# Opening of a two-layer hybrid DeltaNet and diffusion step on one Trainium2 core: x in four loads, squares summed on TensorE, first modulation in fp32 by column groups, first two weight units in two rounds of four k-tiles

## Chip, cores and metric

The kernel runs on one core of a Trainium2 chip. The metric is the device time of one execution in microseconds (us); three runs of the kernel before gave a median of 1513.23 us (1513.16 to 1515.1).

## What is computed

Two groups of tokens, 512 latent and 128 context tokens of width 1024, go through two layers with the same weights. Only the very beginning matters here:

```python
x_lat = x_sample + sincos_2d(rows, GRID_W, D_MODEL)
mod = silu(cond) @ w_ada[layer] + b_ada[layer]
shift1, scale1, gate1, shift2, scale2, gate2 = split(mod, 6)
h = rmsnorm(x, norm_mix_g[layer]) * (1 + scale1) + shift1
p = h @ w_in
```

`cond` is one vector per group (two in all), so `mod` has two columns. After that come a short convolution, a gated delta rule, the output projection, a convolutional feed-forward, and the second layer.

## The kernel before

All activations lie transposed: channels on the 128 partitions, tokens along the free axis. `x` is `[128, 8, 640]`, that is 8 k-tiles of 128 channels by 640 tokens (512 latent, 128 context). A product of full accuracy is made of three fp32r products: each weight tile and each activation is split into a high part (a rounding to fp32r) and a low part (the rest), and TensorE adds hi·hi, hi·lo and lo·hi. A *unit* is one 128-column block of a weight matrix, 8 k-tiles long; it takes 8 k-tiles x 3 products x 2 halves of 320 tokens = 48 matmuls (`products`, L682). The input projection has units 0 to 27.

The opening, everything ahead of unit 0, runs so. SyncE issues one queue of DMAs in this order (L460 to L470): `cols` (small constants, 343.5 KB), the position tables, all of `x` in one transfer (2560 KB), `const`, the first 16 column tiles of `w_ada` in four transfers of 2048 KB each, the first two units of `w_in` (`raw`, 512 KB each), then `cond_rows` and two row tiles. VectorE adds the positions tile by tile (L1549), ScalarE squares each tile (L1051) and VectorE adds the squares to `acc` (L1416), two tiles in flight. TensorE sums `acc` and the last square over the partitions with a matrix of ones in fp32 (`norm_sums(0)`, L714); ScalarE makes `rstd` from it (L1020, L1022).

The first modulation (shift1 and scale1 of layer 0) is worked out in 16 steps: ScalarE rounds a slot of 1024 weights per partition (`ada_hi`, L1066), VectorE subtracts (L1576), TensorE multiplies with 4 stationary columns, the two conditions in high and low parts (`ada`, L694, 8 matmuls of 256 columns a slot). After each pair of slots ScalarE copies the 4 rows out of PSUM (L1072) and TensorE turns them into columns with small fp32 matmuls against `sel` (`ada_columns`, L705). There are four pairs of split buffers, and `ada_hi(n)` waits for the matmuls of slot n-4.

Then ScalarE and VectorE split the weights of units 0 and 1 (L1090, L1570), VectorE multiplies x by `rstd` (L1475), adds the bias and folds the norm gain (L1462, L1468), ScalarE scales and shifts tile by tile (`modulate`, L1036) and rounds (L1043), and VectorE forms the low part (L1479). Unit 0 waits for each k-tile as it comes; unit 1 follows with all eight there. Behind it ScalarE's program has the SiLU of `cond_rows` (L1094), and then for each unit `take` (PSUM to SBUF, L1101), `weight_hi` (L1112) and `silu` (L1106); VectorE's has `conv` (L1514 to L1523), `weight_lo(u + 2)` (L1570) and from unit 1 on a row sum (L1500). Unit u + 2 can begin when its weights are split:

```python
for u in range(NQK):
    take(u, u % 2, u)
    weight_hi(u + 2)
    silu(u % 2, u, u)
```

Of the kernel before, what the change touches and what calls it, by code (L numbers as in the profile page):

```python
# [26 lines left out]
P = 128  # L27
D = 1024
KD = D // P
# [6 lines left out]
HALF = W // 2  # L36
# [5 lines left out]
ADA_COLS = 2 * P  # L42
# [27 lines left out]
for _name, _n in (("norm_mix", 2 * KD * 2), ("norm_ffn", 2 * KD * 2), ("pool_scale", KD * 2),  # L70
                  ("final", KD), ("tap_qkv", 3 * NQKV), ("tap_b", 3 * NB), ("tap_ffn", 2 * 3 * NF),
                  ("o_norm", 1), ("a_log", NT * 8), ("dt_bias", NT * 8), ("w_ba", KD * 16),
                  ("cond", KD * 2), ("b_ada", 96 * 2), ("sel", 2)):
# [72 lines left out]
def build(nc, t):  # L146
    ctx = ExitStack()
    with ctx:
# [17 lines left out]
        silu_c = sb("silu_c", [P, KD, 2])  # L166
        c_parts = sb("c_parts", [P, 2, KD, 4], F32R)
        warm = sb("warm", [P, 1])
        ada_rows = sb("ada_rows", [4, ADA_COLS])
# [17 lines left out]
        sq = [work[:, 6, :], work[:, 7, :]]  # L187
        acc = work[:, 8, :]
# [6 lines left out]
        def heads(ap, n):  # L195
# [47 lines left out]
        ada_first = nc.alloc_sbuf_tensor_at("ada_first", [P, ADA_FIRST, SLOT], F32, offset=off_m)  # L243
        pe_tab = nc.alloc_sbuf_tensor_at("pe_tab", [P, 4, ROWS + GRID_W], F32, offset=off_h)
        more = [nc.alloc_sbuf_tensor_at(f"more{j}", [P, SLOT], F32R, offset=off_h + 2048 + j * SLOT * 4)
                for j in range(8)]
        assert ADA_FIRST * SLOT * 4 <= o4 - off_m
# [47 lines left out]
        s_x = sem("x_loaded")  # L295
# [11 lines left out]
        s_c_parts = sem("c_parts_ready")  # L307
        s_ada_hi = sem("ada_hi")
        s_ada_lo = sem("ada_lo")
# [8 lines left out]
        s_sq = sem("squares_ready")  # L318
        s_acc = sem("squares_added")
# [116 lines left out]
        def ada_row(n):  # L436

            return ps[0:4, (4, 5)[n // 2 % 2], 0:ADA_COLS]

        def ada_split(n):  # L440

            return more[n % 4], more[4 + n % 4]
# [5 lines left out]
        def _(sp):  # L448
# [13 lines left out]
            sp.dma_start(x[:], t["x"]).then_inc(s_x, 16)  # L462
            sp.dma_start(const[:], t["const"]).then_inc(s_const, 16)
            n = ADA_FIRST // 4
            for q in range(4):
                sp.dma_start(ada_first[:, n * q:n * (q + 1), :],
                             t["w_ada"][n * q:n * (q + 1)].rearrange("u p f -> p u f")).then_inc(s_ada1[q], 16)
# [204 lines left out]
        def _(pe):  # L672
# [15 lines left out]
            def ada(n):  # L688

                s = n % 2  # L690
                pe.wait_ge(s_ada_lo, n + 1)
                for k in range(4):
                    for q, w in enumerate(ada_split(n)):
                        last = nc.tensor.matmul(ada_row(n), c_parts[:, q, 4 * s + k, :],  # L694
                                                w[:, k * ADA_COLS:(k + 1) * ADA_COLS],
                                                start=(s == 0 and k == 0 and q == 0),
                                                stop=(s == 1 and k == 3 and q == 1))
                last.then_inc(s_ada_pe, 1)

            def ada_columns(g):  # L700

                pe.wait_ge(s_ada_cp, g + 1)
                for h in range(2):
                    at = ADA_COLS + 2 * (2 * g + h)
                    last = nc.tensor.matmul(ps[:, 0, at:at + 2], ada_rows[:, h * P:(h + 1) * P],  # L705
                                            col("sel")[0:4], start=True, stop=True)
                last.then_inc(s_ada_t, 1)
# [1375 lines left out]
```

## Time and profile before

| what | value |
|---|---|
| median of three runs | 1513.23 us |
| span of the profiled execution, first to last instruction | 1508.5 us |
| TensorE busy over the span | 1403.6 us (93%) |
| VectorE, ScalarE, GpSimd busy | 988.2, 430.7, 496.7 us |
| mean granted TensorE clock | 0.982 |
| DMA traffic | 163.24 MB, 31% of 16 engines |

The profiled execution's own time is given by its span; the median of the runs is 4.7 us above it, which is what lies around the span. A busy time is the sum of an engine's instructions; time in which TensorE is idle is lost only where nothing else could have been done there.

### The profile page before, as it was taken

The page shows a single profiled execution, that of the slowest core. Times are in us where ns is not written, and L with a number is a line of the kernel's source. Part 1 is how long each engine was busy: PE and PEld are TensorE (multiplying, and loading weights), DVE is VectorE, ACT ScalarE, POOL GpSimd, SP SyncE. Part 2 cuts the span into 40 slices and gives each one's busy share as a digit, 9 for nine tenths or more (in the row PEclk, how much of TensorE's full clock was granted, in tenths as well). Part 3 has the DMA queues.
Part 4 walks back from the last instruction along what each step waited for, and adds up shares of the span by engine and source line. Part 5 has one row for each costly group of instructions (what it writes and reads, how often), then busy time and mean ns, then how long its engine had stood idle before and what let it go on. Part 6 is the DMA issues. An engine that isn't in the chain of part 4 may idle for free.

```text
span 1508.5 us, 24564 instructions
## 1 busy us (share of the span) xinstructions
PE 1403.6 (93%) x9517; PEld 1366.5 (91%) x9517; DVE 988.2 (66%) x1405; ACT 430.7 (29%) x748; POOL 496.7 (33%) x300
## 2 busy tenths in 40 slices
PE   2799999989888899999999999878999999999996
PEld 1599989989788799999999999768999999999995
DVE  5774689887675777778788886447774155325554
ACT  4834443364421532102310321344110011001122
POOL 0000010003225133453356334113544545445442
PEclk9899999999989999999999999999999999999998
DMA  9342211353032244343434442111332222222222
GB/s 371 123 154 84 99 56 71 139 173 133 15 129 84 84 138 177 129 159 115 150 117 167 138 136 73 54 42 56 111 107 75 70 83 68 73 82 70 69 72 82
DMA packets 44791, 163.24 MB, mean 108 GB/s; under 512 B 4800, under 2 KB 5952, under 8 KB 43584
## 3 DMA queue, kind: packets, MB, share of 16 engines
q1 hardware_dynamic: 44736, 162.52, 31.1%
q8 instruction: 32, 0.52, 0.1%
q14 instruction: 23, 0.19, 0.0%
HBM read 154.12 MB, written 6.82 MB: 107 GB/s over the span
## 4 chain that ended last, share of the span: by engine, by line
PE 82%; DVE 8%; ACT 4%; issue 3%; DMA 2%; ACTq 0%; POOL 0%; DVEq 0%; SPq 0%; POOLq 0%
PE ps L682 73%; PE ps L967 1%; ACT work L1036 1%; ACT work L1184 1%; DMA x<-in_x 1%; PE ps L714 1%; PE ps L790 1%; DMA work<-in_zeros 1%; DVE wlo L1570 1%; PE ps L921 1%; PE ps L919 1%; PE ps L909 1%; PE ps L760 1%; PE ps L694 1%; DVE work L1416 1%
## 5 line engine op out<-in xcount | busy, mean ns | idle before, releaser
L682 PE MATMUL ps<-hhi,whi 128*128 128x320 f32 x1984 | 458.7, 312 | 29.4 <-DVE hlo L1479 27.4
L682 PE MATMUL ps<-hlo,whi 128*128 128x320 f32 x1984 | 453.9, 310 | 0.0
L682 PE MATMUL ps<-hhi,wlo 128*128 128x320 f32 x1984 | 453.2, 310 | 0.0
L682 PEld LDWEIGHTS ps<-hhi,whi 128*128 128x128 f32 x1984 | 333.6, 189 | 37.3 <-issue 23.9
L682 PEld LDWEIGHTS ps<-hlo,whi 128*128 128x128 f32 x1984 | 334.2, 189 | 0.0
L682 PEld LDWEIGHTS ps<-hhi,wlo 128*128 128x128 f32 x1984 | 333.7, 189 | 0.0
L603 POOL TENSOR_TENSOR wlo<-raw,whi 128x1024 fp32r<-128x1024 f32 (+1 forms) x100 | 249.7, 2497 | 8.3
L600 POOL TENSOR_SCALAR whi<-raw 128x1024 fp32r<-128x1024 f32 (+1 forms) x100 | 102.9, 1029 | 401.7 <-PE ps L682 360.5
L608 POOL TENSOR_TENSOR wlo<-raw,whi 128x1024 fp32r<-128x1024 f32 x44 | 110.2, 2504 | 214.2 <-ACT whi L1387 214.2
L682 PE MATMUL ps<-hidlo,whi 128*128 128x320 f32 x704 | 160.3, 308 | 0.0
L682 PE MATMUL ps<-hidhi,wlo 128*128 128x320 f32 x704 | 160.2, 308 | 0.0
L682 PE MATMUL ps<-hidhi,whi 128*128 128x320 f32 x704 | 160.2, 308 | 0.0
L1394 ACT ACTIVATE work<-ps 128x640 f32<-128x640 f32 x44 | 31.1, 706 | 429.0 <-PE ps L682 429.0
L1924 DVE TENSOR_TENSOR hidlo<-work,hidhi 128x640 fp32r<-128x640 f32 (+1 forms) x44 | 107.1, 2434 | 41.2 <-ACT hidhi L1404 41.2
L1517 DVE SCALAR_TENSOR_TENSOR work<-work,cols 128x511 f32<-128x511 f32 x120 | 122.3, 1060 | 3.7 <-DVE work L1514 0.3
L1514 DVE TENSOR_SCALAR work<-work,cols 128x640 f32<-128x640 f32 x60 | 60.2, 1003 | 97.0 <-ACT work L1394 79.5
L1500 DVE SCALAR_TENSOR_TENSOR ada_raw<-ada_raw,cond_rows 128x1024 bf16<-128x1024 f32 x70 | 121.7, 1738 | 0.0
L682 PEld LDWEIGHTS ps<-hidhi,wlo 128*128 128x128 f32 x704 | 117.8, 188 | 0.0
L682 PEld LDWEIGHTS ps<-hidlo,whi 128*128 128x128 f32 x704 | 117.8, 188 | 0.0
L682 PEld LDWEIGHTS ps<-hidhi,whi 128*128 128x128 f32 x704 | 117.7, 188 | 0.0
L1399 ACT ACTIVATE work<-work 128x640 f32<-128x640 f32 x44 | 32.5, 739 | 216.9 <-DVE work L1523 216.9
L1451 DVE SCALAR_TENSOR_TENSOR x<-ps,mod,x 128x320 f32<-128x320 f32 (+2 forms) x120 | 45.4, 434 | 70.5 <-PE ps L682 70.5
(197 smaller groups left out, 1403.6 us busy)
## 6 DMA issues: line engine op xcount, KB each, us to landing
raw<-in_w_gu SPq DMA_DIRECT2D x88, 512.0 KB, 3.2
ada_raw<-in_w_rows SPq DMA_DIRECT2D x70, 512.0 KB, 3.4
raw<-in_w_in SPq DMA_DIRECT2D x28, 512.0 KB, 3.3
raw<-in_w_dn SPq DMA_DIRECT2D x32, 448.0 KB, 3.3
ada_first<-in_w_ada SPq DMA_DIRECT2D x4, 2048.0 KB, 22.7
raw<-in_w_dn SPq DMA_DIRECT2D x16, 512.0 KB, 3.3
row_late<-in_w_rows SPq DMA_DIRECT2D x10, 512.0 KB, 3.3
raw<-in_w_out SPq DMA_DIRECT2D x8, 512.0 KB, 4.3
```

Of the source, the lines that this page charges most:

```text
L600: nc.gpsimd.tensor_scalar(whi[s][:, 0:n], raw[s][:, 0:n], 1.0, 0.0, ALU.mult, ALU.add).then_inc(s_whi, 1)
L603: nc.gpsimd.tensor_tensor(wlo[s][:, 0:n], raw[s][:, 0:n], whi[s][:, 0:n].bitcast(F32), ALU.subtract).then_inc(s_split, 1)
L608: nc.gpsimd.tensor_tensor(wlo[s][:], raw[s][:], whi[s][:].bitcast(F32), ALU.subtract).then_inc(s_split, 1)
L682: last = nc.tensor.matmul(pair[pr][:, b], wt[s][:, cs], act[:, k, b * HALF:(b + 1) * HALF], start=(j == 0 and q == 0), stop=(j == len(tile ...
L694: last = nc.tensor.matmul(ada_row(n), c_parts[:, q, 4 * s + k, :], w[:, k * ADA_COLS:(k + 1) * ADA_COLS], start=(s == 0 and k == 0 and q = ...
L1394: nc.scalar.activation(halves(pad[0]), pair["A"], ACT.Copy).then_inc(s_ev["A"], 1)
L1399: nc.scalar.activation(cv[1], cv[0], ACT.Silu).then_inc(s_silu, 1)
L1451: last = nc.vector.scalar_tensor_tensor(out=x[:, k, xc:xc + ln], in0=pair[n][:, bk, pc:pc + ln], scalar=mod[:, layer, 3 * part + 2, k, cd: ...
L1500: last = nc.vector.scalar_tensor_tensor(out=(row_out(n), row_buf(n)[:, 0:SLOT // 2].bitcast(mybir.dt.bfloat16))[c], in0=row_buf(n), scalar ...
L1514: own.tick(nc.vector.tensor_scalar(dst[:, 0:W], src[:, 0:W], taps[1], None, ALU.mult))
L1517: last = nc.vector.scalar_tensor_tensor(out=dst[:, c0 + 1:c0 + n], in0=src[:, c0:c0 + n - 1], scalar=taps[0], in1=dst[:, c0 + 1:c0 + n], o ...
L1924: nc.vector.tensor_tensor(hidlo[:, i, :], h32[0], hidhi[:, i, :].bitcast(F32), ALU.subtract).then_inc(s_hid, 1)
```

## The change

`x` comes in four transfers of two k-tiles, the first ahead of `const`; `cols` comes after `x`, then the two `raw` units, and only then `w_ada`, again in four transfers of 2048 KB, now grouped as two halves (`half`) of 4 k-tiles of shift and scale each. Positions go tile by tile as the transfers land. The squares are no longer added on VectorE: each of the 8 squared tiles is summed by TensorE in fp32 (16 matmuls instead of 4).

The split of the first `w_ada` tiles goes. `c_cols` holds the two conditions in the first 2 of 32 columns for every k-tile (the rest zeros), and fp32 matmuls of 512 columns write PSUM partitions 0, 32, 64 or 96 onward: shift or scale (`b`) times first or second half of the contraction (`part`). There are 16 of them in each half. One copy and four fp32 matmuls with `sel` (which adds the two parts) give the columns of a half; bias and fold are done per half.

Odd k-tiles are modulated by VectorE, even ones by ScalarE, all in buffers of their own. Units 0 and 1 run in two rounds: k-tiles 0 to 3 of both, then the second half of the modulation, then k-tiles 4 to 7 of unit 0 and of unit 1. `weight_lo(2)` goes ahead of the convolution of unit 0. Semaphore counts elsewhere are shifted to match.

```diff
-        silu_c = sb("silu_c", [P, KD, 2])
...
+        first_sq = sq + cv
+        first_h = pad + h32 + cv + sq
...
-        ada_first = nc.alloc_sbuf_tensor_at("ada_first", [P, ADA_FIRST, SLOT], F32, offset=off_m)
+        ada_first = nc.alloc_sbuf_tensor_at("ada_first", [P, 2, 2, 4, 2, ADA_SPAN], F32, offset=off_m)
+        ada_end = off_m + ADA_FIRST * SLOT * 4
+        ada_rows = nc.alloc_sbuf_tensor_at("ada_rows", [P, 2, ADA_SPAN], F32, offset=ada_end)
...
                 sp.sem_inc(sm, PRIMED)
+            sp.dma_start(pe_tab[:], t["pe"]).then_inc(s_pe, 16)
+            sp.dma_start(x[:, 0:2], t["x"][:, 0:2]).then_inc(s_x[0], 16)
+            sp.dma_start(const[:], t["const"]).then_inc(s_const, 16)
+            for j in range(1, 4):
+                sp.dma_start(x[:, 2 * j:2 * j + 2], t["x"][:, 2 * j:2 * j + 2]).then_inc(s_x[j], 16)
             sp.dma_start(cols[:], t["cols"]).then_inc(s_cols, 16)
-            sp.dma_start(pe_tab[:], t["pe"]).then_inc(s_pe, 16)
...
             for s in range(2):
                 sp.dma_start(raw[s][:], t["w_in"][s]).then_inc(s_raw[s], 16)
+            for half in range(2):
+                for q in range(2):
+                    sp.dma_start(ada_first[:, half, q], t["w_ada"][half, q]).then_inc(s_ada1[2 * half + q], 16)
...
-            def ada(n):
...
+            def first_sums():
+                pe.wait_ge(s_const, 16)
+                for k in range(KD):
+                    pe.wait_ge(s_sq, k + 1)
+                    for b in range(2):
+                        last = nc.tensor.matmul(pair["X"][:, b], ones, first_sq[k % 4][:, b * HALF:(b + 1) * HALF],
+                                                start=(k == 0), stop=(k == KD - 1))
+                    last.then_inc(s_first_sums, 1)
+            def ada(half):
+                for q in range(2):
+                    pe.wait_ge(s_ada1[2 * half + q], 16)
+                    for i in range(2):
+                        for b in range(2):
+                            for part in range(2):
+                                row = BLOCK * (2 * b + part)
+                                last = nc.tensor.matmul(ada_bank(half)[row:row + BLOCK], c_cols[:, 4 * part + 2 * q + i, :],
+                                                        ada_first[:, half, q, 2 * part + i, b, :],
+                                                        start=(q == 0 and i == 0), stop=(q == 1 and i == 1))
                 last.then_inc(s_ada_pe, 1)
-            def ada_columns(g):
...
+            def ada_columns(half):
+                pe.wait_ge(s_ada_cp, half + 1)
+                for i in range(4):
+                    last = nc.tensor.matmul(first_mods(half)[:, 4 * i:4 * i + 4], ada_rows[:, half, i * P:(i + 1) * P],
+                                            col("sel"), start=True, stop=True)
                 last.then_inc(s_ada_t, 1)
             def norm_sums(q):
-                for part, (src, sm, n) in enumerate(((acc, s_acc, 8 * (q + 1)), (sq[1], s_sq, 8 * (q + 1)))):
+                for part, (src, sm, n) in enumerate(((acc, s_acc, 8 * q), (sq[1], s_sq, 8 * (q + 1)))):
                     pe.wait_ge(sm, n)
                     for b in range(2):
                         last = nc.tensor.matmul(pair["X"][:, b], ones, src[:, b * HALF:(b + 1) * HALF],
                                                 start=(part == 0), stop=(part == 1))
                 last.then_inc(s_norm, 1)
-            pe.wait_ge(s_const, 16)
...
+            def first_units(s, ks):
+                for k in ks:
+                    pe.wait_ge(s_h, PRIMED + k + 1)
+                    for q, (wt, act) in enumerate(((whi, hhi), (whi, hlo), (wlo, hhi))):
+                        for b in range(2):
+                            last = nc.tensor.matmul(pair["AB"[s]][:, b], wt[s][:, k * P:(k + 1) * P],
+                                                    act[:, k, b * HALF:(b + 1) * HALF],
+                                                    start=(k == 0 and q == 0), stop=(k == KD - 1 and q == 2))
+                return last
+            first_sums()
+            pe.wait_ge(s_silu_c, 1)
+            ada(0)
+            ada_columns(0)
+            for k in range(4):
+                for s in range(2):
+                    if k == 0:
+                        pe.wait_ge(s_split, s + 1)
+                    first_units(s, [k])
+            ada(1)
+            ada_columns(1)
+            for s in range(2):
+                first_units(s, range(4, KD)).then_inc(s_unit, 1)
...
             for u in range(28):
-                in_unit(u, u // 2, u % 2, (lambda j: pe.wait_ge(s_h, PRIMED + j + 1)) if u == 0 else None)
+                if u >= 2:
+                    in_unit(u, u // 2, u % 2)
...
-            def ada_hi(n):
...
+            def weight_hi(u):
+                act.wait_ge(s_raw[u % 2], u // 2 * 16 + 16)
+                act.wait_ge(s_unit, u - 1)
+                nc.scalar.activation(whi[u % 2][:], raw[u % 2][:], ACT.Copy).then_inc(s_whi, 1)
+            def first_square(k):
+                act.wait_ge(s_x0, k + 1)
+                if k >= 4:
+                    act.wait_ge(s_first_sums, k - 3)
+                nc.scalar.activation(first_sq[k % 4], x[:, k, :], ACT.Square).then_inc(s_sq, 1)
+            def first_modulate(k):
+                act.wait_ge(s_first_fold, k // 4 + 1)
+                act.wait_ge(s_a, k + 1)
+                for c0, n, cd in RANGES:
+                    last = nc.scalar.activation(first_h[k][:, c0:c0 + n], first_h[k][:, c0:c0 + n], ACT.Identity,
+                                                bias=mod[:, 0, 0, k, cd:cd + 1], scale=mod[:, 0, 1, k, cd:cd + 1])
+                last.then_inc(s_first_mod[0], 1)
+            def first_hi(k):
+                act.wait_ge(s_first_mod[k % 2], k // 2 + 1)
+                nc.scalar.activation(hhi[:, k, :], first_h[k], ACT.Copy).then_inc(s_hi, 1)
+            for k in range(6):
+                first_square(k)
             act.wait_ge(s_cols, 16)
-            nc.scalar.activation(silu_c[:], cond, ACT.Silu).then_inc(s_silu_c, 1)
...
+            act.wait_ge(s_c_zero, 1)
+            nc.scalar.activation(c_cols[:, :, 0:2], cond, ACT.Silu).then_inc(s_silu_c, 1)
+            for k in range(6, KD):
+                first_square(k)
+            rsqrt_of_sums(0)
+            for s in range(2):
+                act.wait_ge(s_raw[s], 16)
+                nc.scalar.activation(whi[s][:], raw[s][:], ACT.Copy).then_inc(s_whi, 1)
+            for half in range(2):
+                act.wait_ge(s_ada_pe, half + 1)
+                nc.scalar.activation(ada_rows[:, half, :], ada_bank(half), ACT.Copy).then_inc(s_ada_cp, 1)
+                for k in range(4 * half, 4 * half + 4, 2):
+                    first_modulate(k)
+                    first_hi(k)
+                    first_hi(k + 1)
...
-            def add_batch():
...
+            def add_batch(half):
+                src = first_mods(half).rearrange("p (i b c) -> p b i c", i=4, b=2)
+                bias = b_ada[:, 0:16, :].rearrange("p (b k) c -> p b k c", b=2)
+                ks = slice(4 * half, 4 * half + 4)
+                dve.wait_ge(s_ada_t, half + 1)
+                nc.vector.tensor_tensor(mod[:, 0, 0:2, ks, :], src, bias[:, :, ks, :], ALU.add).then_inc(s_mod, 1)
+                dve.wait_ge(s_mod, half + 1)
+                v = mod[:, 0, 1, ks, :]
+                nc.vector.scalar_tensor_tensor(out=v, in0=v, scalar=1.0, in1=g_mix[:, 0, ks, :],
+                                               op0=ALU.add, op1=ALU.mult).then_inc(s_first_fold, 1)
...
-            clear_acc(0)
...
+            nc.vector.memset(c_cols[:], 0.0).then_inc(s_c_zero, 1)
             dve.wait_ge(s_pe, 16)
             def add_position(k):
                     tab = pe_tab[:, k - KD // 2, ROWS:].unsqueeze(1).to_broadcast([P, ROWS, GRID_W])
                 nc.vector.tensor_tensor(v, v, tab, ALU.add).then_inc(s_x0, 1)
-            for k in range(2):
+            for k in range(KD):
+                if k % 2 == 0:
+                    dve.wait_ge(s_x[k // 2], 16)
                 add_position(k)
-            for i in range(KD // 2):
...
             dve.wait_ge(s_const, 16)
             nc.vector.tensor_scalar(below[:], const[:, 1:3, :], -1.0, 1e30, ALU.add, ALU.mult).then_inc(s_masks, 1)
             nc.vector.tensor_copy(ident16[:], ident).then_inc(s_masks, 1)
                 nc.vector.tensor_tensor(wlo[u % 2][:], raw[u % 2][:], whi[u % 2][:].bitcast(F32),
                                         ALU.subtract).then_inc(s_split, 1)
-            for n in range(ADA_FIRST):
...
+            def first_normed(k):
+                nc.vector.tensor_tensor(first_h[k], x[:, k, :], rstd, ALU.mult).then_inc(s_a, 1)
+            def first_modulate(k):
+                dve.wait_ge(s_a, k + 1)
+                dve.wait_ge(s_first_fold, k // 4 + 1)
+                for c0, n, cd in RANGES:
+                    last = nc.vector.tensor_scalar(first_h[k][:, c0:c0 + n], first_h[k][:, c0:c0 + n],
+                                                   mod[:, 0, 1, k, cd:cd + 1], mod[:, 0, 0, k, cd:cd + 1],
+                                                   ALU.mult, ALU.add)
+                last.then_inc(s_first_mod[1], 1)
+            def first_lo(k):
+                dve.wait_ge(s_hi, k + 1)
+                nc.vector.tensor_tensor(hlo[:, k, :], first_h[k], hhi[:, k, :].bitcast(F32),
+                                        ALU.subtract).then_inc(s_h, 1)
             weight_lo(0)
             weight_lo(1)
-            apply_norm(0, 0)
+            dve.wait_ge(s_rstd, 1)
+            for k in range(4):
+                first_normed(k)
+            for half in range(2):
+                add_batch(half)
+                first_modulate(4 * half + 1)
+                first_modulate(4 * half + 3)
+                for k in range(4 * half, 4 * half + 4):
+                    first_lo(k)
+                if half == 0:
+                    for k in range(4, KD):
+                        first_normed(k)
...
+                if u == 0:
+                    weight_lo(2)
                 conv(pad[s], cv[s], [tap_qkv[:, j, u:u + 1] for j in range(3)])
-                weight_lo(u + 2)
+                if u:
+                    weight_lo(u + 2)
```

On the host `w_ada` is laid out so that each transfer reads one run of 16 KB per partition, and `sel` has 4 columns over 128 rows.

## Rows read from the trace of the kernel before

**Rows 1.** The page: busy time, share and instructions of each engine.

```profile
PE 1403.6 (93%) x9517; PEld 1366.5 (91%) x9517; DVE 988.2 (66%) x1405; ACT 430.7 (29%) x748; POOL 496.7 (33%) x300
```

**Rows 2.** Stages: start:end length, busy (count) PE, PEld, DVE, ACT, POOL; clock, DMA share, GB/s.

```profile
0.00:25.60 25.60, 0.00 (x0) 0.01 (x1) 11.67 (x24) 7.31 (x11) 0.20 (x4) 1.00 0.91 352
25.60:59.60 34.00, 25.04 (x168) 16.48 (x168) 25.23 (x29) 26.25 (x36) 0.00 (x0) 0.92 0.61 231
...
70.30:173.00 102.70, 102.67 (x675) 97.44 (x675) 59.34 (x97) 47.65 (x62) 3.03 (x2) 1.00 0.34 118
```

**Rows 3.** Chain that ended last, 0 to 220 us: start us, us, what.

```profile
2.17 11.60 DMA x<-in_x
...
25.62 4.62 PE ps L714 x8
...
34.09 1.07 PE ps L694 x8
...
39.38 1.07 PE ps L694 x8
...
55.03 0.11 DVE mod L1462
...
70.33 37.23 PE ps L682 x252
```

**Rows 4.** Stages of the loads; columns as in rows 2.

```profile
0.00:3.00 3.00, 0.00 (x0) 0.00 (x0) 0.68 (x3) 1.28 (x1) 0.20 (x4) 1.00 0.22 59
3.00:13.00 10.00, 0.00 (x0) 0.00 (x0) 0.44 (x4) 0.22 (x1) 0.00 (x0) 1.00 0.98 363
13.00:25.00 12.00, 0.00 (x0) 0.00 (x0) 9.94 (x15) 5.21 (x8) 0.00 (x0) 1.00 1.02 412
```

**Rows 5.** Timeline of SyncE's queue; the view of DMA issues, 12 to 30 us.

```profile
15.95 7.19 SPq L469 DMA_DIRECT2D raw<-in_w_in  x2
...
raw<-in_w_in SPq DMA_DIRECT2D x2, 512.0 KB, 20.8
```

**Rows 6.** Groups by line and shape, 0 to 105 us: busy us, mean ns | idle before.

```profile
L694 PE MATMUL ps<-more,c_parts 128*4 128x256 f32 x128 | 17.3, 282 | 2.5 <-DVE more L1576 2.5
...
L1479 DVE TENSOR_TENSOR hlo<-work,hhi 128x640 fp32r<-128x640 f32 x8 | 6.5, 822 | 3.3 <-ACT hhi L1043 3.3
...
L1043 ACT ACTIVATE hhi<-work 128x640 f32 x8 | 5.4, 720 | 0.0
...
L1101 ACT ACTIVATE work<-ps 128x640 f32<-128x640 f32 x5 | 3.5, 699 | 10.7 <-PE ps L682 10.7
```

**Rows 7.** Stages around the first unit, columns as in rows 2; chain, 136 to 139 us.

```profile
54.10:59.60 5.50, 0.00 (x0) 0.00 (x0) 2.94 (x7) 3.86 (x7) 0.00 (x0) 0.50 0.98 324
59.60:64.30 4.70, 4.64 (x16) 4.32 (x17) 4.14 (x6) 4.61 (x9) 0.00 (x0) 0.50 0.87 372
...
136.31 2.15 PE ps L760 x8
```

**Rows 8.** Timeline: start us, us, engine line op, out<-in xcount [idle before].

```profile
53.07 0.60 PE L705 MATMUL ps<-cols,ada_rows 4*128 4x2 f32 x4 [0.46 <-ACT ada_rows L1072]
...
55.74 2.29 ACT L1036 ACTIVATE work<-work,mod 128x512 f32<-128x512 f32 x4 [2.72 <-DVE mod L1468]
...
59.19 2.43 ACT L1036 ACTIVATE work<-work,mod 128x512 f32<-128x512 f32 x4
...
59.66 0.87 PE L682 MATMUL ps<-hhi,whi 128*128 128x320 f32 x2 [5.99 <-DVE hlo L1479]
...
70.06 1.28 ACT L1094 ACT_TABLE_LOAD   x1
...
71.36 1.91 ACT L1094 ACTIVATE cond_rows<-cond_rows 128x2048 f32<-128x2048 f32 x1
...
73.95 0.55 DVE L1514 TENSOR_SCALAR work<-work,cols 128x640 f32<-128x640 f32 x1 [2.94 <-ACT cond_rows L1094]
...
76.52 1.22 DVE L1570 TENSOR_TENSOR wlo<-raw,whi 128x1024 fp32r<-128x1024 f32 x1
```

More of the change, by code:

```diff
@@ L41 @@
 NF = D_FF // P
-ADA_COLS = 2 * P
+ADA_SPAN = 4 * P
 ADA_FIRST = 16
@@ L72 @@
                   ("o_norm", 1), ("a_log", NT * 8), ("dt_bias", NT * 8), ("w_ba", KD * 16),
-                  ("cond", KD * 2), ("b_ada", 96 * 2), ("sel", 2)):
+                  ("cond", KD * 2), ("b_ada", 96 * 2), ("sel", 4)):
     COLS[_name] = (_at, _n)
@@ L294, in build @@
         s_cols = sem("cols_loaded")
-        s_x = sem("x_loaded")
+        s_x = [sem(f"x_loaded{j}") for j in range(4)]
         s_const = sem("const_loaded")
@@ L318, in build @@
         s_sq = sem("squares_ready")
+        s_first_sums = sem("first_squares_summed")
         s_acc = sem("squares_added")
@@ L433, in build, with ada_bank, first_mods @@
         O_BANKS = (0, 1, 6, 7)
[L436 to L442, printed above, removed]
+        def ada_bank(half):
+            return ps[:, 4 + half, :]
+        def first_mods(half):
+            return ps[:, 7, 384 + 16 * half:400 + 16 * half]
         block = ctx.enter_context(nc.Block())
@@ L686, in products @@
                 return last
-            def ada(n):
[L690 to L697, printed above, removed]
-                last.then_inc(s_ada_pe, 1)
@@ L700, in ada_columns @@
-            def ada_columns(g):
[L702 to L706, printed above, removed]
+            def first_sums():
[6 more added lines that the diff above has]
+                    last.then_inc(s_first_sums, 1)
@@ L1075, in _ @@
-            act.wait_ge(s_cols, 16)
-            nc.scalar.activation(silu_c[:], cond, ACT.Silu).then_inc(s_silu_c, 1)
-            squares(0, (s_x0, s_x0), ((0, 2), (1, 2)))
-            for n in range(4):
-                ada_hi(n)
-                if n == 1:
-                    rsqrt_of_sums(0)
-            for g in range(ADA_FIRST // 2):
-                ada_copy(g)
-                for n in (2 * g + 4, 2 * g + 5):
-                    if n < ADA_FIRST:
-                        ada_hi(n)
-                    elif n < ADA_FIRST + 2:
-                        s = n - ADA_FIRST
-                        act.wait_ge(s_raw[s], 16)
-                        nc.scalar.activation(whi[s][:], raw[s][:], ACT.Copy).then_inc(s_whi, 1)
@@ L1106, in silu @@
                 nc.scalar.activation(qkv[:, m, :], cv[s], ACT.Silu).then_inc(s_silu, 1)
-            def weight_hi(u):
-                act.wait_ge(s_raw[u % 2], u // 2 * 16 + 16)
-                act.wait_ge(s_unit, u - 1)
-                nc.scalar.activation(whi[u % 2][:], raw[u % 2][:], ACT.Copy).then_inc(s_whi, 1)
             for u in range(NQK):
@@ L1529, in _ @@
             nc.vector.memset(scale_col, -0.5 * float(np.log(DK))).then_inc(s_fill, 1)
-            clear_acc(0)
-            dve.wait_ge(s_silu_c, 1)
-            for q in range(2):
-                own.tick(nc.vector.tensor_copy(c_parts[:, q, :, 0:2], silu_c[:]))
-            nc.vector.memset(c_parts[:, 1, :, 2:4].bitcast(F32), 0.0)
-            own.sync()
-            nc.vector.tensor_tensor(c_parts[:, 0, :, 2:4], silu_c[:], c_parts[:, 0, :, 0:2].bitcast(F32),
-                                    ALU.subtract).then_inc(s_c_parts, 1)
-            dve.wait_ge(s_x, 16)
+            nc.vector.memset(c_cols[:], 0.0).then_inc(s_c_zero, 1)
             dve.wait_ge(s_pe, 16)
@@ L2012 @@
     w_ada = np.concatenate([a["w_ada"][0], a["w_ada"][1]], axis=1)
-    groups = w_ada[:, :ADA_FIRST * P].reshape(2, 4, P, ADA_FIRST // 2, ADA_COLS)
-    arrays["w_ada"] = np.ascontiguousarray(groups.transpose(3, 0, 2, 1, 4).reshape(ADA_FIRST, P, SLOT))
+    groups = w_ada[:, :ADA_FIRST * P].reshape(2, 2, 2, P, 2, 2, ADA_SPAN)
+    arrays["w_ada"] = np.ascontiguousarray(groups.transpose(5, 1, 3, 0, 2, 4, 6).reshape(2, 2, P, 4, 2, ADA_SPAN))
     arrays["w_rows"] = np.ascontiguousarray(w_ada.T.reshape(96, P, D)[ADA_FIRST:])
@@ L2032 @@
         "cond": np.stack([chunks(a["c"][0]), chunks(a["c_ctx"])], axis=-1),
-        "sel": (np.arange(P)[:, None] % 2 == np.arange(2)[None, :]).astype(np.float32),
+        "sel": (np.arange(P)[:, None] % (2 * BLOCK) % BLOCK + np.arange(P)[:, None] // (2 * BLOCK) * 2
+                == np.where(np.arange(P)[:, None] % BLOCK < 2, np.arange(4)[None, :], -1)).astype(np.float32),
         "b_ada": twice(chunks(a["b_ada"].reshape(-1))),
```

90 lines of the change are left out of this document (20 added, 70 removed).

## Prediction

> **What bounds the kernel now.** I read the page first: TensorE is busy 93% of the span [rows 1], so a change pays where TensorE stands idle or does work that can go. The stage view says where that is [rows 2]. From 70.3 us on TensorE is busy 102.67 of 102.70 us, with VectorE at 59.34 and ScalarE at 47.65: this stretch is bound by TensorE alone, and an earlier start of it shifts all that follows. Ahead of it lie 25.6 us without a matmul and 34 us in which TensorE's 25 busy us are no unit work. The chain shows what sets their length [rows 3]: x's load until 13.8 us, squares until 25.6, their sum in 4.62 us, then turns of 5.3 us for four slots of weights (34.09 to 39.38, and so on) in which split, subtract and matmul release each other, then the modulation at 55, and from 70.33 matmuls without a gap. Unit 0 starts at 59.66 [rows 8] and is fed tile by tile. A unit matmul costs 37.23/252 = 0.148 us [rows 3]. At 70.33 there are 12 of unit 0 and 48 of unit 1 to go, so unit 1 ends at 70.33 + 60 x 0.148 = 79.2 us. That is the mark: the change is worth what it moves the end of unit 1, less what the later units then wait.
>
> **The loads.** Until 3 us 0.18 MB have moved, then 363 GB/s until 13 us (3.81 MB in all), then 412 [rows 4]. x and what was issued ahead of it is 3.12 MB, reached at 11.1 us; it landed at 2.17 + 11.60 = 13.8 [rows 3]: a lag of 2.7. The first two weight units (12.82 MB) are reached at 34.9 and landed at about 37, 20.8 us after their issue [rows 5]: a lag of 2.1. With these, in the new order: first x part (0.80 MB) at 7.4 us, last (3.03) at 13.6, cols at 14.5, raw (4.43) at 17, the two transfers of the first half of w_ada (6.53 and 8.63) at 22.2 and 27.3, those of the second at 32 and 37. The lag may be 1.5 us more or less.
>
> **Squares.** Added are 12 fp32 matmuls, in pairs of records: the sum took 4.62/8 = 0.577 us a record at the start [rows 3], while the same shape takes 2.15/8 = 0.269 at 136 us [rows 7]. The stage view prints 0.92 for the clock of 25.6 to 59.6 [rows 2], yet by duration TensorE began at its half level (1.2 GHz): the print is no proof at the start. Even so, tiles at 2.1 us, then 1.1, end by 18 us. rstd, both weight splits and four normed tiles follow by 25. All of it lies under the loads, and so do the table load for SiLU and the later cols. Removed from ScalarE and VectorE are 16 passes each; they were the turn's length, not work left on the path.
>
> **First half of the modulation.** It waits for 27.3 us. The price of an fp32 matmul of 512 columns into one group of 32 is shown nowhere before. A record would be 0.269 x 512/320 = 0.43 us at the high clock, two records 0.86. Bounds: 0.22 if four groups run at once, 0.86 if none overlap. I take 0.43, one record's time: the two records of one matmul use the same group and come one after the other, so with matmuls in order only the second record of one can lie beside the first of the next. At half clock double. TensorE has stood idle since 18 us, so it starts low: the clock view has 4.70 us at 0.50 after the restart of 59.6 [rows 7]. The first 8 matmuls from 22.2 end near 28, the next 8 at the high clock near 31.8.
> The Trainium skill, "TensorE: Matmul & The Clock Gate", section "Packing small matmuls", gives 2.38 times for three column groups and a span of one matmul plus some 4 ns a tile; by it a group of four would cost one matmul, and the sum would be 1499. The same section says that weight loads overlap running matmuls only where row groups differ, which here they never do; by that nothing overlaps, 1516. Against the latter, the weight loads of full rows are busy 97.44 us beside matmuls busy 102.67 of 102.70 [rows 2].
>
> **From there to the first unit matmul.** Copy out of PSUM, 0.7 (128x640 takes 0.699 [rows 6]; at most 0.3 less). Four fp32 matmuls with sel, 8 records: 0.15 each by the small ones (four in 0.60 [rows 8]), at most 0.27 [rows 7]; I take 1.1 and 0.3 for the start: 1.4, at most 2.4. Bias and fold until ScalarE starts: 55.03 [rows 3] to 55.74 [rows 8], 0.7. Then 3.92 us passed until 59.66 with two modulated tiles ahead of the first rounding; four activations for two tiles take 2.43 [rows 8], so with one tile fewer it is 2.7. Sum 5.5 to 5.6: k-tile 0 at 37.4. VectorE's tile 1 (0.55 by the tensor_scalar of [rows 8]) lies under ScalarE's tile 0. Four tiles cost ScalarE 2.43 + 4 x 0.72 [rows 6] = 5.3, VectorE 4 x 0.82 in low parts: faster than TensorE.
>
> **Round one.** 48 matmuls, clock low again (it stood at 0.50 from 54.1 [rows 7] with TensorE idle): 4.7 us at 0.267 (320 columns at 1.2 GHz) are 17.6, the other 30.4 at 0.148 take 4.5: 46.6.
> **Second half.** 16 matmuls and a last record: 17 x 0.43 = 7.3: 53.9. Bounds 3.4 and 13.7. Hand-overs again 5.6, with TensorE idle: 59.5. Round two: unit 0's 24 in 4.7 + 0.95, unit 1's 24 in 3.55: 68.7. That is 10.5 ahead of 79.2.
>
> **What waits next.** Unit 1 now takes 3.55 instead of 7.1 us behind unit 0. ScalarE is done with tile 7 near 62, then cond_rows' table load and SiLU (1.28 + 1.91 [rows 8]) until 65.2, take(0) 0.7, weight_hi(2) about 1.05, and VectorE's weight_lo(2) 1.22 [rows 8]: 68.1, just ahead of 68.7. Were weight_lo(2) still behind the convolution (73.95 to 76.52 [rows 8], 2.6) it would cost 2. Behind it stand conv(0), silu(0), take(1), weight_hi(3), conv(1), weight_lo(3): 2.6 + 0.7 + 0.7 + 1.05 + 2.6 + 1.2 less overlaps, near 75.9, against unit 2's end at 75.8: 0.2 lost. Each later unit needs less than 7.1 us of VectorE. SyncE's queue moves loads of units 2 and 3 and the x save earlier; they lie behind w_ada and end before 55.
> Sum: 10.5 - 0.2 = 10.3 off the span, 1498.2. The median is 4.7 over the span, so 1503.0.
>
> **Rivals.**
> Four groups at once (0.22): first half ends at 30.7 with part still low, second 3.9 earlier; with part of it eaten by the clock the gain is 14.3, so 1499. For it: different groups, different stationary data, nothing in common but rows. Against: the two records of each matmul. If the clock stays high between the bursts, up to 4 more, 1495.
> No overlap (0.86), the other side: TensorE does the first half from 22.2 until 38.1 and the second in 13.7, unit 1 ends at 81.4, and with the stall the time is 1515.7. It decides from about 0.8 us a matmul. For it: one stream of columns through the same rows. If the clock stayed low for these matmuls too, 11 and 14 us more. Against that: the 4-column matmuls of 256 columns take 1.07/8 = 0.134 us [rows 3], less than the 0.213 of 256 cycles at 1.2 GHz.
> A new wait: the loads land later, sel's matmuls cost 0.27, or units 2 and 3 wait for VectorE. 3 to 5 us less gain: 1507.
>
> **How the numbers follow.** One record's time each, 0.42; four at once, 0.29; a new wait, 0.14; no overlap, 0.12; anything else, as that the groups are not what the code says or that later stages give time back, 0.03. A measurement of this kernel tells about 0.2% (3 us) from no change. The range takes in the first three with their bounds, 1495 to 1509. Faster by over 0.2%: 0.42 + 0.29 + 0.13 + some of the rest, 0.85; within it, most of no overlap, 0.08; slower 0.07.
>
> **What would show it.** Right: first matmul of unit 0 near 37.4, w_ada landing at 27 and 37, records of the column-group matmuls starting 0.43 apart per matmul, round one near 46.6, unit 1's end near 68.7, and units from 3 on without a gap. Wrong: starts 0.86 apart, loads that land out of order, a TensorE idle of over 1 us between units 1 and 4, or the same span from 70 us on growing longer.

## The result, and the profile after

The changed kernel takes 1494.68 us (median of 4 runs, 1493.26 to 1494.81) against 1513.2 before; the ratio is 0.9875, 95% interval 0.9863 to 0.9886. It is 18.5 us faster where 10.2 were forecast, and 0.3 us outside the range. Its profiled execution took 1494.65 us with a span of 1492.9: 1.75 us lie around the span, not 4.7.

The chain of the changed kernel over the opening (start us, us, what), to be held against [rows 3]:

```profile
6.32 18.27 DMA ada_first<-in_w_ada
24.63 2.73 PE ps L707 x16
27.38 0.61 ACT ada_rows L1126
28.03 1.88 PE ps L716 x8
...
30.35 1.21 ACT work L1105 x2
...
33.32 9.97 PE ps L735 x48
43.29 3.62 PE ps L707 x32
46.93 0.61 ACT ada_rows L1126
47.58 1.07 PE ps L716 x8
...
51.96 5.77 PE ps L735 x24
...
67.38 1.14 DVE wlo L1586
68.57 21.38 PE ps L683 x144
```

One long load now sets the first 24.6 us; squares, rstd and weight splits lie under it. Then come the first half of the modulation, round one (33.32), the second half (43.29), a wait and round two (51.96). Unit 2 starts at 60.93 without a wait, unit 3 at 68.57 after one of 0.6 us. Before, unit 1 ended at 79.2 and a unit takes 7.05 us, so unit 3 started at 86.2: it is 17.6 us earlier now.

The same view says how the column groups run. A record of 512 fp32 columns is worth 0.43 us; 32 of them pass in 3.62 us, four to each 0.45. The weight loads show the pattern (timeline, loads of TensorE):

```profile
43.22 0.16 PEld L707 LDWEIGHTS ps<-ada_first,c_cols 128*32 128x32 f32 x8 [0.18 <-issue]
43.68 0.13 PEld L707 LDWEIGHTS ps<-ada_first,c_cols 128*32 128x32 f32 x4 [0.30 <-issue]
44.10 0.13 PEld L707 LDWEIGHTS ps<-ada_first,c_cols 128*32 128x32 f32 x4 [0.30 <-issue]
```

After the first eight they come in fours, one set every 0.43 us, the time of one record: four groups at once.

Stages of the loads (columns as in [rows 2]), to be held against [rows 4]:

```profile
3.00:13.00 10.00, 5.35 (x12) 3.60 (x13) 5.49 (x11) 4.18 (x6) 0.00 (x0) 1.00 1.00 386
13.00:25.00 12.00, 7.94 (x41) 4.29 (x44) 4.23 (x8) 7.48 (x10) 0.00 (x0) 1.00 1.02 433
```

386 and 433 GB/s in place of 363 and 412.

The spans differ by 15.6 us, not by 17.6: 2.0 us come back later, in several pieces. Here is the first place, the wait ahead of the first grams, as stages of the changed kernel and then of the kernel before:

```profile
172.40:175.00 2.60, 0.05 (x2) 0.03 (x1) 2.52 (x4) 2.60 (x10) 0.00 (x0) 1.00 0.61 202
175.00:179.00 4.00, 4.00 (x18) 3.28 (x19) 3.12 (x5) 2.07 (x5) 0.00 (x0) 0.60 0.16 43
```

```profile
190.00:192.50 2.50, 0.00 (x0) 0.00 (x0) 2.48 (x4) 2.50 (x10) 0.00 (x0) 1.00 0.62 210
192.50:196.50 4.00, 3.96 (x23) 2.80 (x23) 3.06 (x5) 2.08 (x5) 0.75 (x1) 1.00 0.19 61
```

TensorE is idle for the same 2.5 us in both, waiting for VectorE. Behind it the granted clock is 0.60 in the one and 1.00 in the other, and the grams and decay rows take 3.03 and 1.54 us instead of 2.05 and 0.86. By 222.57 (238.50 before) the lead is 15.9.

The second place adds to the lead. It is the wait for a load of zeros; the changed kernel first, then the kernel before:

```profile
263.77 7.83 DMA work<-in_zeros
...
305.62 1.94 PE ps L877 x16
```

```profile
279.68 9.12 DMA work<-in_zeros
...
322.76 1.94 PE ps L850 x16
```

The same transfer of 2048 KB takes 1.3 us less, and the lead is 17.1 at the second row of each. It takes 9.0 to 9.1 us in all three profiles with the opening of before and 7.7 to 8.5 in all eleven with the new one or a variant of it; why is not shown. From there longer stretches of half clock around 400 and 960 us bring the lead to 16.7 and then to 15.7, where it stays to the end.

### The profile page after: what moved, and what is told of

It is laid out like the page before. It is cut to its first block, busy times and chain, and to the rows that moved or that the text cites. A ratio compares the mean times of both kernels' runs of the same rounds, so it can differ in the third digit from the quotient of the medians.

```text
span 1492.9 us, 24317 instructions
## 1 busy us (share of the span) xinstructions
PE 1406.8 (94%) x9461; PEld 1367.8 (92%) x9461; DVE 967.6 (65%) x1388; ACT 411.3 (28%) x719; POOL 498.7 (33%) x300
## 4 chain that ended last, share of the span: by engine, by line
PE 83%; DVE 7%; ACT 4%; issue 3%; DMA 2%; SPq 0%; ACTq 0%; POOL 0%; DVEq 0%; POOLq 0%
PE ps L683 73%; PE ps L994 2%; DMA ada_first<-in_w_ada 1%; PE ps L735 1%; ACT work L1215 1%; ACT work L1064 1%; PE ps L816 1%; DVE wlo L1586 1%; PE ps L948 1%; PE ps L946 1%; PE ps L936 1%; PE ps L786 1%; DMA work<-in_zeros 1%; DVE qkv L1669 1%; PE ps L806 1%
## 5 line engine op out<-in xcount | busy, mean ns | idle before, releaser
L683 PE MATMUL ps<-hhi,whi 128*128 128x320 f32 x1952 | 451.0, 312 | 20.3 <-DVE hlo L1514 18.2
L683 PE MATMUL ps<-hlo,whi 128*128 128x320 f32 x1952 | 446.8, 310 | 0.0
L683 PE MATMUL ps<-hhi,wlo 128*128 128x320 f32 x1952 | 446.7, 310 | 0.0
L683 PEld LDWEIGHTS ps<-hhi,whi 128*128 128x128 f32 x1952 | 328.4, 189 | 27.3 <-issue 18.3
L683 PEld LDWEIGHTS ps<-hlo,whi 128*128 128x128 f32 x1952 | 328.5, 189 | 0.0
L683 PEld LDWEIGHTS ps<-hhi,wlo 128*128 128x128 f32 x1952 | 328.3, 189 | 0.0
```

The lines of the kernel that those rows point to most:

```text
L683: last = nc.tensor.matmul(pair[pr][:, b], wt[s][:, cs], act[:, k, b * HALF:(b + 1) * HALF], start=(j == 0 and q == 0), stop=(j == len(tile ...
```

## Experiments

Times are medians; the kernel before gave 1513.74, 1513.48 and 1513.03 us in the three sets. The changed kernel was not in these sets, so a kernel is set against it by the two ratios to the kernel before, and by the times at which the same work starts in the two profiles.

### Group order

```diff
                 for q in range(2):
                     pe.wait_ge(s_ada1[2 * half + q], 16)
-                    for i in range(2):
-                        for b in range(2):
-                            for part in range(2):
+                for b in range(2):
+                    for part in range(2):
+                        for q in range(2):
+                            for i in range(2):
```

> The 16 column-group matmuls of a half in an order in which all four of one group stand together, both transfers waited for first; the same arithmetic. If different groups run beside each other only where they are neighbours in the program, with matmuls in order, a half costs 4 + 3 x 3 = 13 matmul times of 0.86 us = 11.2 us at the high clock in place of 3.6: second half 7.6 us longer, first half about 11 longer (nothing done ahead of 24.6, partly at the low clock), total some 15 to 20 us slower than the changed kernel, near or above the kernel before. If a matmul with 32 stationary columns is simply cheap (0.226 us) in whatever order: second half 3.6 as now, total within 2 us of the changed kernel.

1507.12 us, ratio 0.9961 (0.9943 to 0.998). The chain:

```profile
24.70 10.79 PE ps L708 x32
...
50.23 8.80 PE ps L708 x32
```

The same 32 records take 8.80 us instead of 3.62 when neighbours belong to one group, so order matters, and a matmul of 32 stationary columns is not simply cheap. But the first theory, matmuls strictly in order, gave 11.2 and not 8.80, and 15 to 20 us in all where the ratios and medians say 12 to 13. The weight loads tell more (timeline):

```profile
51.04 0.11 PEld L708 LDWEIGHTS ps<-ada_first,c_cols 128*32 128x32 f32 x1 [0.32 <-issue]
51.47 0.11 PEld L708 LDWEIGHTS ps<-ada_first,c_cols 128*32 128x32 f32 x1 [0.32 <-issue]
51.90 0.14 PEld L708 LDWEIGHTS ps<-ada_first,c_cols 128*32 128x32 f32 x3 [0.32 <-issue]
52.33 0.14 PEld L708 LDWEIGHTS ps<-ada_first,c_cols 128*32 128x32 f32 x2 [0.29 <-issue]
```

One load per 0.43 us for the first four steps, then about two per step until 56.7, then one again for four: 20 steps of 0.43 are 8.7 us. That is what comes out when each group has 8 records in a row and the next group begins four records before the last one ends: 8 + 3 x 4 = 20. So a record of a free group starts while three records of a busy group still stand ahead of it in the program. In the changed kernel's order (two records of group 0, of 1, of 2, of 3) the last group has to pass three waiting records, which just fits. The first half of this run, from 24.67 us on and in part at the low clock, has the same pattern of loads. The depth of three rests on these two stretches of one kernel.

### x in one load

```diff
-            sp.dma_start(x[:, 0:2], t["x"][:, 0:2]).then_inc(s_x[0], 16)
+            sp.dma_start(x[:], t["x"]).then_inc(s_x[0], 16)
...
-            for j in range(1, 4):
-                sp.dma_start(x[:, 2 * j:2 * j + 2], t["x"][:, 2 * j:2 * j + 2]).then_inc(s_x[j], 16)
...
                 if k % 2 == 0:
-                    dve.wait_ge(s_x[k // 2], 16)
+                    dve.wait_ge(s_x[0], 16)
```

> x in one transfer in the place of its first part. If the squares lie under the loads of w_ada, as the prediction has it, the first matmul of the modulation waits for w_ada at the same 19.8 and 24.6 us, squares end near 22 and rstd near 24; VectorE's four normed tiles end by 28, before the columns; no change in time (within 0.5 us). If the four parts earn something of their own (the rival): k-tile 0 is ready after 33.3 us by the 2 to 5 us that x comes later.

1495.52 us, ratio 0.9879 (0.9859 to 0.9898): no difference that can be told from the changed kernel's 0.9875. The chain shows a small one:

```profile
1.71 9.29 DMA x<-in_x
...
12.70 10.45 PE ps L693 x32
...
25.71 2.36 DVE wlo L1584 x2
28.07 2.94 DVE work L1589 x4
...
34.31 9.75 PE ps L733 x48
```

The squares now end at 23.2 and the path runs through them, rstd, the weight splits and the four normed tiles. Round one starts at 34.31, 1.0 us later. The four parts bring 1.0 us at this place, 0.65 at unit 3 (69.22 against 68.57), and nothing that the times show. At round one the expectation of nothing was too low, that of 2 to 5 us too high.

### w_ada in runs of 4 KB

```diff
-sp.dma_start(ada_first[:, half, q], t["w_ada"][half, q])
+sp.dma_start(ada_first[:, half, q], t["w_ada"][half, q].rearrange("j p b f -> p j b f"))
```

The layout in HBM is changed to match.

> w_ada laid out in HBM so that a transfer reads four runs of 4 KB per partition in place of one of 16 KB. The loads landed 2.7 us earlier than predicted from the kernel before, whose runs were of 4 KB. If the run length is the cause, the second transfer lands near 27 in place of 24.6 us and the time is about 2 us longer. If the order of the loads is (x and const ahead, nothing else waiting), no change.

1494.84 us, ratio 0.9876 (0.9856 to 0.9896): no difference from the changed kernel. In the chain and the stages:

```profile
25.47 3.44 PE ps L707 x16
```

```profile
13.00:23.00 10.00, 7.82 (x38) 4.30 (x36) 2.32 (x7) 7.72 (x10) 0.00 (x0) 1.00 1.03 410
```

The rate falls from 436 to 410 GB/s (13 to 23 us), which is the kernel before's 410 to 412, and the second transfer lands 0.8 us later. So the run length is a cause, of 0.8 us out of the 2.7 by which the loads came ahead of the prediction. Some 0.3 us more come from what moved before 13 us. The rest, 1.6 us, is the lag between the time at which the bytes are reached by rate and the landing: 1.0 to 1.1 us in this kernel and in the changed one, 2.1 to 2.7 before. The run of x in one load bears on it too: there the matmuls that wait for the second transfer begin at 24.92 us, at 437 GB/s, so the four parts of x make at most 0.3 us of it. The order of the loads is left as a rival and was not tried. The 0.8 us have shrunk to 0.3 at unit 3 (68.87).

### weight_lo(2) behind the convolution

```diff
-                if u == 0:
-                    weight_lo(2)
                 conv(pad[s], cv[s], [tap_qkv[:, j, u:u + 1] for j in range(3)])
-                if u:
-                    weight_lo(u + 2)
+                weight_lo(u + 2)
```

> weight_lo(2) again behind the convolution of unit 0, all else as changed. By the prediction's chain unit 2 starts 1.5 us later (62.4 in place of 60.9), but unit 3, which waits for weight_lo(3) at 68.6 now, only about 0.9 later: 0.9 us slower in all. If the wait of unit 3 hides it: no change.

1493.66 us, ratio 0.9864 (0.9845 to 0.9884). The chain after ScalarE's SiLU of cond_rows:

```profile
60.65 1.15 DVE wlo L1586
61.84 28.28 PE ps L683 x191
```

Unit 2 starts 0.9 us later, but unit 3 follows without a wait, at 68.9 against 68.57. That is the second of the two expectations: the wait of unit 3 hides it. This part of the change is worth 0.3 us at unit 3 and nothing that the times show.

### One round

```diff
             ada(0)
             ada_columns(0)
+            ada(1)
+            ada_columns(1)
             for k in range(4):
...
-            ada(1)
-            ada_columns(1)
```

> Both halves of the modulation, then k-tiles 0 to 3 of units 0 and 1, then 4 to 7 of unit 0 and of unit 1: the two rounds undone. TensorE waits for the last transfer of w_ada (near 34.5 us) and starts the units near 42.5, but then has one ramp of the clock and no idle between rounds: 96 matmuls in about 16.3 us, unit 1's end near 59 in place of 61. If the two rounds earn time (the change's reading), this is slower by 5 or more; if not, it is equal or up to 2 us faster, the wait of unit 3 for weight_lo(3) deciding.

1488.94 us, ratio 0.9844 (0.983 to 0.9857): near 5 us faster than the changed kernel, where at best 2 were expected. The chain:

```profile
7.13 28.34 DMA ada_first<-in_w_ada
35.52 3.39 PE ps L707 x16
...
39.58 1.05 PE ps L716 x8
40.63 10.68 PE ps L735 x72
...
62.15 21.38 PE ps L683 x144
```

TensorE waits for the last load until 35.5, but ScalarE and VectorE have made tiles 0 to 3 ready by then, so the matmuls begin at 40.63, at once behind the columns, and run on. The low clock is passed before them: granted are 0.50 from 35.5 to 37.3 us, under the column groups, and 1.00 from 39.5 on, so the 72 unit matmuls take 0.148 us each from the start. From the last landing to the first unit matmul only 5.1 us pass. In the changed kernel round one ends at 43.3, and behind it stand the second half's 3.6 us and another 5.1 of hand-overs, in which TensorE is idle but for the columns' 1.1. The two rounds, as the change orders them, cost 6.4 us at unit 3 (68.57 against 62.15).

### The second half inside round one

```diff
             for k in range(4):
                 for s in range(2):
...
                     first_units(s, [k])
-            ada(1)
-            ada_columns(1)
+                if k == 0:
+                    ada(1)
+                elif k == 1:
+                    ada_columns(1)
```

> The second half of the modulation inside round one: its matmuls after k-tile 0 of both units, its columns after k-tile 1. The 5.2 us in which TensorE is idle between the rounds (46.8 to 52.0) and the second stretch at the low clock (4.5 us at 0.27 in place of 0.148) go: unit 1's end near 55 in place of 61. Units 2 and 3 then wait for ScalarE and VectorE: unit 3 starts near 63.4 in place of 68.6, 5 us faster in all. If the last transfer of w_ada lands after 40, or the split of weights holds everything, under 2 us.

1487.05 us, ratio 0.9823 (0.981 to 0.9837), 26 us faster than the kernel before and 7 to 8 faster than the changed one. The chain:

```profile
33.57 3.54 PE ps L735 x12
37.10 4.19 PE ps L707 x32
41.30 1.96 PE ps L735 x12
43.26 0.80 PE ps L716 x8
...
54.48 1.22 DVE wlo L1588
...
63.50 21.39 PE ps L683 x144
```

TensorE goes from 33.57 to the end of unit 1 almost without a gap, and unit 3 starts 5.1 us earlier, as expected. The time is lower by more than that: the low stretch behind the first grams is missing in this profile (1.65 us), and about 1 us is not traced.

### Unit 3's weights ahead

```diff
-            for u in range(NQK):
+            for u in range(2):
+                take(u, u, u)
+                weight_hi(u + 2)
+            silu(0, 0, 0)
+            cond_silu()
+            silu(1, 1, 1)
+            for u in range(2, NQK):
...
+                if u == 0:
+                    weight_lo(3)
```

> take(1) and the split of unit 3's weights go ahead of silu(0) on ScalarE and of conv(1) on VectorE, and the SiLU of cond_rows goes behind silu(0). Unit 3 then starts when unit 2 ends, near 68.0 in place of 68.6, and unit 2 no later: 0.6 us faster. If unit 3's wait is not on the path: no change.

1492.76 us, ratio 0.9869 (0.9854 to 0.9884). One row of the chain, 60.62 to 88.78:

```profile
60.62 28.16 PE ps L683 x192
```

192 matmuls without a wait: unit 3 starts at 67.7, 0.9 us earlier, where 0.6 was expected. The ratio is lower by about the same, which is within the interval.

### Both

The edits of the last two runs together.

> mid and lo3 together. Unit 1's end near 55, unit 2 without a wait, unit 3 near 62: 6.5 us faster than the changed kernel. If the two overlap in what they gain: 5 us, as mid alone.

1487.25 us, ratio 0.9825 (0.9811 to 0.9838): equal to the second half inside round one alone. The chain has 192 matmuls from 55.42 on:

```profile
55.42 28.16 PE ps L683 x192
```

Unit 3 starts at 62.5, 1.0 ahead of the kernel with the second half inside round one alone, and at VectorE's products (158.65 us against 159.96) it leads by 1.3. Then this profile has a low stretch at the gap and that one has none, and by 215.9 both are level. Against the changed kernel 6.5 us were expected and 7.5 came; the difference between the two orders is smaller than what the clock does to either.

### The gap filled

```diff
                     if GRAMS_AFTER[u] == 0:
+                        for _ in range(3):
+                            nc.tensor.matmul(ps[:, 6, :], ones, const[:].rearrange("p a b -> p (a b)"),
+                                             start=True, stop=True)
                         pe.wait_ge(s_l2, 8)
```

> The kernel before, with three idle fp32 matmuls of 512 columns (2.6 us at the high clock, into a PSUM bank that is overwritten next) in the wait ahead of the first grams, where TensorE stands idle for 2.5 us (190.0 to 192.5). The gap did not lower the clock in the profile of before and did in that of the changed kernel. If this gap is what makes runs of before differ (1509.3 to 1515.1), the spread shrinks and the median falls by up to 1.7 us. If other low stretches make the spread, it stays.

> The same three matmuls in the changed kernel. The 3.4 us at half clock behind the gap (grams and decay rows 3.03 and 1.54 us in place of 2.05 and 0.86) go: 1.6 us faster, median near 1493. If the clock falls elsewhere instead, no change.

> The same three matmuls in the kernel with both reorderings. That kernel was 1.3 us ahead of the one with the second half inside round one alone, until it lost 1.7 us at half clock behind the same gap; without the gap it should come to 1485.5, 9 us under the changed kernel.

Before with the filling: 1511.46 us, ratio 0.9989 (0.998 to 0.9997), 12 runs from 1508.12 to 1513.28. The median falls by 1.6 us and the interval just leaves out no change, although neither profile of the kernel before is low behind this gap; some of its executions may be, but no profile shows one. The spread stays at 5 us, so this gap is not what makes it. Changed with the filling: 1490.87 us, ratio 0.9852 (0.9834 to 0.9869), 3 to 4 us below the changed kernel's, though the two intervals overlap slightly. 1.6 us were expected. Its profile has the low stretch gone:

```profile
68.85 21.39 PE ps L683 x144
...
221.20 21.14 PE ps L683 x144
```

From unit 3 to this row are 152.35 us; in the changed kernel 222.57 - 68.57 = 154.00. The 1.65 us are those of the half clock. What the median fell beyond them is not explained. Both with the filling: 1487.52 us, ratio 0.9833 (0.9819 to 0.9848), no gain in the median where 1485.5 was expected, though the low stretch is gone here too and the profiled span of 1484.4 is the shortest of all. So the cost of this one stretch is shown, and that it can be avoided; that avoiding it pays in every kernel is not.

### The kernel before once more

> The kernel before once more, for a second profile. The first has a span of 1508.5 us, 3 under the usual 1511.5. If runs differ by stretches at half clock, this profile shows a further one or two of 3.4 us (1.7 us each) where the first has none, and the opening up to 70.3 us stands within 1 us. If the opening itself varies, part of the change's gain against the median lies there.

1513.72 us, span 1511.9. Stages of the first profile of before, then of this one (columns as in [rows 2]):

```profile
200.00:410.00 210.00, 199.19 (x1517) 192.47 (x1516) 166.90 (x365) 93.65 (x264) 28.11 (x48) 1.00 0.28 98
...
970.00:1040.00 70.00, 53.77 (x293) 47.58 (x294) 37.18 (x53) 41.07 (x66) 10.33 (x6) 0.89 0.09 30
```

```profile
200.00:410.00 210.00, 199.33 (x1496) 192.89 (x1495) 166.01 (x362) 91.59 (x251) 28.14 (x48) 0.98 0.28 98
...
970.00:1040.00 70.00, 51.84 (x271) 44.42 (x270) 34.83 (x50) 42.33 (x68) 9.39 (x6) 0.85 0.07 23
```

Unit matmuls without a gap begin at 70.22 against 70.33, and at 238.39 against 238.50: the opening varies by 0.1 us. From 448.49 to 450.84 it is 2.35 us behind instead of 0.1 ahead, and at 1035.08 against 1031.67 it is 3.4 behind; the granted clock is 0.98 and 0.85 in these stages where the first profile has 1.00 and 0.89. The 3.4 us by which the two spans differ are late and come with the clock.

## Why the prediction was right and wrong

**Where the time would go: right.** The mark was the end of unit 1, and what is won there carries through the TensorE-bound stretch; 17.6 us at unit 3 are still 17.6 at VectorE's products (182.60 before, 165.04 after). Squares, rstd, splits and the positions of x all lie under the loads.

**First half of the modulation: the step that failed first.** I had matmuls start in order and gave a column-group matmul 0.43 us, one record's time. It costs 3.62/16 = 0.226: the four groups run at once. The second half took 3.62 in place of 7.3, and of the first half 2.7 us were left after the last landing where I had 4.5. That is 5.5 us. The group order run shows that matmuls are not held to their order in the program, as I had assumed: that gave 11.2 us for the grouped records, and they took 8.80. By the reading given there, a record passes up to three that wait for their group. The rival of four at once, which I had at 1499 and 0.29, was the case. The Trainium skill ("TensorE: Matmul & The Clock Gate", section "Packing small matmuls") has this overlap, one matmul's time for the group, and the trace agrees with that. Its sentence that weight loads pass running matmuls only with other row groups does not hold here: all four groups use every row, and their loads stand together under running matmuls.

**Loads: the step that failed second, 2.7 us too late.** I took rate and lag from the kernel before. The second transfer landed at 24.6, not 27.3; 0.8 of it is the longer run per partition, 0.3 a higher rate before 13 us, and 1.6 a shorter lag, whose cause stays open.

**Hand-overs and clock: near.** 33.32 - 27.36 = 5.96 against 5.6 for the first, with the columns at half speed (1.88 us, against 1.4), and 5.05 against 5.6 for the second. Round one took 9.97 against 9.2, round two 8.97 against 9.2. Both began at half clock as in [rows 7], but by the granted clock for about 6.0 and 4.4 us where I had 4.7 for each. The clock staying high between the bursts did not occur.

**What waits next: near.** Unit 2 without a wait, unit 3 with 0.6 against 0.2. Putting weight_lo(2) first, which I held worth 2 us at unit 2, is worth 0.9 there and 0.3 at unit 3.

**The sum.** Unit 1 ended at 60.9 against 68.7: 7.8 us, made of 2.7 for loads and 5.5 for the groups, less 0.4 of smaller terms. Less 0.4 of wait, that makes 17.6 out of 10.3. In the sum for the time, 7.3 us more at unit 3, 2.0 given back behind it and 2.9 too much in what I added for the way from span to median make the 8.3 us from 1503.0 to 1494.7.

**What took it out of the range.** Its low end was 18.2 us below the median before: four groups at once and a clock that stays high, with loads as in the kernel before. The clock did not stay high, but the loads came earlier, which no rival had: 17.6 us. The other 0.9 of the 18.5 lie behind unit 3, which I had at nothing. The first profile of before is a quick execution: it is 2.9 us under the median once 1.75 us around the span are counted, so my 4.7 for what lies around a span was two things in one. Against that profile the changed kernel gives 2.0 of its 17.6 us back; against the second profile, whose opening is the same within 0.1 us and whose span is 1511.9, it is 19.0 ahead. 2.35 us of that difference were lost by the second profile between 238 and 450 us, where its granted clock is 0.98 (200 to 410 us). The clock alone does not make the 0.9: added up over stages of 4 us, the time at half clock behind unit 3 is 45 us in the first profile of before, 54 in the second and 54 in the changed kernel. The load of zeros, 1.3 us shorter than in either profile of before, lies in this part too. That later stretches can move the difference of two kernels by 1 us or more either way was not among my bounds.

**What I did not see.** I worked out the two rounds as they stand and did not ask what one round would give. TensorE's two idle stretches and two ramps of the clock were in my sum; with tiles 0 to 3 made ready while the last load comes, one round without them is 5 us faster than the changed kernel, and the second half inside round one 7.5. The changed kernel's gain is thus not one of its rounds; the rest of its new opening earns it.

## What to carry to other kernels

When a phase waits for a load, ask what else can be ready when it lands: here splitting TensorE's work into rounds around a wait cost more, in hand-overs and in a second ramp of the clock, than starting early gained, while putting the dependent matmuls inside a running stretch was the fastest of the three. Narrow fp32 matmuls are cheap when they are spread over column groups, neighbours in different groups. And before a span is turned into a median, take two profiles: the difference can be as large as the terms one argues about.

## What was not expected of the hardware

Matmul records of different column groups run four at once, and not strictly in the order of the program (32 records: 3.62 us in the interleaved order, 8.80 with eight of a group in a row). That a record starts past up to three waiting ones of busy groups is the reading that gives 20 steps of 0.43 us; no other depth was tried.

The same 2.5 us of idle TensorE is followed by 3 to 4 us at half clock in six of the eleven profiles without filling and by none in five, both of the kernel before among them; the stretch costs 1.6 us in the changed kernel. Stretches elsewhere go with how executions of the kernel before differ: the second profile is 3.4 us longer and has 9 us more at half clock, and of eight other executions the longest span (1514.4 us) has a mean clock of 0.975 and the shortest (1508.4) 0.983.

The view of the clock can print full clock where durations say half: at the first matmuls of the kernel before a record of 320 fp32 columns takes 0.577 us [rows 3] against 0.269 later [rows 7]. In the changed kernel the view prints 1.00 from 7 to 12 us, while the weight loads of such records start 0.53 us apart (8.31 to 11.51 us).
